# Part of the weights' low parts moved to VectorE, and earlier first quads, in the feed-forward products of two transformer blocks

## What is computed

```python
def conv_ffn(h, w_up, conv_w, conv_b, w_down):
    u = causal_dwconv(h @ w_up, conv_w, conv_b)
    g, val = jnp.split(u, 2, axis=-1)
    return (jax.nn.silu(g) * val) @ w_down
...
def swiglu(h, w_gate, w_up, w_down):
    return (jax.nn.silu(h @ w_gate) * (h @ w_up)) @ w_down
```

## Time and profile before

| what | value |
|---|---|
| median of 3 runs | 3294.6 us |
| lowest, highest | 3288.72, 3298.83 us |
| profiled execution: span | 3309.4 us |
| profiled execution: time of its own beside the span | the page gives none |
| mean granted TensorE clock | 0.930 |
| TensorE busy | 2912.6 us, 88% |
| GpSimd busy | 2220.5 us, 67%; 2220.1 of it in 884 low parts of 2522 ns on average |
| ScalarE busy | 1167.9 us, 35% |
| VectorE busy | 1128.3 us, 34% |
| moved by DMA | 598.17 MB, mean 181 GB/s |

### The profile page before, as it was taken

How to read it: one execution, slowest core, us unless ns; L and a number is a source line. 1 busy time by engine, 2 the same in 40 slices (tenths; PEclk the granted TensorE clock), 3 DMA queues, 4 the chain that set the end, 5 groups by cost and what they waited for, 6 DMA issues and landing times.

```text
span 3309.4 us, 54043 instructions
## 1 busy us (share of the span) xinstructions
PE 2912.6 (88%) x21608; PEld 2795.5 (84%) x21608; DVE 1128.3 (34%) x1286; ACT 1167.9 (35%) x1286; POOL 2220.5 (67%) x889
## 2 busy tenths in 40 slices
PE   4657879896789999999997976698898999999997
PEld 4657769775779999999997975598798999999997
DVE  4688771256855444422213032302102000001222
ACT  2222223332233433334443443233333333333443
POOL 2455768353758889878884843085476888887885
PEclk8778999798999999999998987698999999999999
DMA  7976765432746666545552542053243554554452
GB/s 218 351 267 241 272 250 207 166 142 81 261 176 226 229 219 238 191 164 179 187 180 90 189 129 90 8 221 129 102 164 129 180 187 179 181 187 165 178 184 96
DMA packets 112195, 598.17 MB, mean 181 GB/s; under 512 B 23340, under 2 KB 25388, under 8 KB 54860
## 3 DMA queue, kind: packets, MB, share of 16 engines
q1 hardware_dynamic: 92736, 570.84, 47.4%
q10 hardware_dynamic: 19340, 25.59, 2.7%
HBM read 581.98 MB, written 14.40 MB: 180 GB/s over the span
## 4 chain that ended last, share of the span: by engine, by line
PE 66%; issue 17%; POOL 11%; DVE 5%; ACT 1%; DMA 1%; ACTq 0%; POOLq 0%; DVEq 0%; SPq 0%
PE ps L825 20%; PE ps L827 20%; PE ps L829 20%; POOL w_lo L358 11%; PE ps L884 2%; PE ps L977 1%; PE ps L950 1%; DVE work L1281 1%; PE ps L966 1%; PE ps L841 0%; PE ps L839 0%; PE ps L843 0%; PE ps L954 0%; DVE work L1383 0%; DVE work L1252 0%
## 5 line engine op out<-in xcount | busy, mean ns | idle before, releaser
L358 POOL TENSOR_TENSOR w_lo<-raw,w_hi 128x1024 fp32r<-128x1024 f32 x884 | 2220.1, 2522 | 1054.5 <-ACT w_hi L379 1052.7
L825 PE MATMUL ps<-a_hi,w_hi 128*128 128x256 f32 x6512 | 1882.4, 289 | 236.9 <-DVE a_lo L1273 113.2
L827 PE MATMUL ps<-a_lo,w_hi 128*128 128x256 f32 x6512 | 1871.8, 287 | 0.0
L829 PE MATMUL ps<-a_hi,w_lo 128*128 128x256 f32 x6512 | 1870.7, 287 | 0.5 <-issue 0.5
L825 PEld LDWEIGHTS ps<-a_hi,w_hi 128*128 128x128 f32 x6512 | 1281.2, 197 | 251.6 <-issue 235.7
L379 ACT CAST w_hi<-raw 128x1024 fp32r<-128x1024 f32 x884 | 916.6, 1047 | 1589.8 <-PE ps L829 1080.8
L827 PEld LDWEIGHTS ps<-a_lo,w_hi 128*128 128x128 f32 x6512 | 1281.5, 197 | 0.2
L829 PEld LDWEIGHTS ps<-a_hi,w_lo 128*128 128x128 f32 x6512 | 1280.0, 197 | 0.7 <-issue 0.7
L1216 DVE SCALAR_TENSOR_TENSOR arena<-arena,small 128x1024 f32<-128x1024 f32 x150 | 388.9, 2628 | 105.4 <-DMA arena<-ada 104.5
L1332 DVE TENSOR_TENSOR a_lo<-arena,a_hi 128x1024 fp32r<-128x1024 f32 x44 | 112.7, 2565 | 364.4 <-ACT a_hi L662 364.4
L1652 DVE TENSOR_TENSOR arena<-ps,work 128x512 f32 (+1 forms) x22 | 15.2, 692 | 488.4 <-ACT work L792 488.4
(11 more groups left out here) (126 smaller groups left out, 1183.9 us busy)
## 6 DMA issues: line engine op xcount, KB each, us to landing
raw<-stream SPq DMA_DIRECT2D x442, 1024.0 KB, 4.8
arena<-ada SPq DMA_DIRECT2D x192, 512.0 KB, 4.6
arena<-memT SPq DMA_DIRECT2D x4, 512.0 KB, 7.9
res<-xT SPq DMA_DIRECT2D x1, 2048.0 KB, 20.8
rel_rows<-arena ACTq DMA_DIRECT2D x1, 2048.0 KB
mem_high<-a_hi ACTq DMA_DIRECT2D x1, 2048.0 KB, 46.6
mem_low<-a_lo ACTq DMA_DIRECT2D x1, 2048.0 KB, 24.6
k_spill<-arena ACTq DMA_DIRECT2D x4, 512.0 KB, 5.7
```

What stands on the lines that cost most here:

```text
L358: pool.tensor_tensor(w_lo[:, slot], raw[:, tile_slot, part * HALF:(part + 1) * HALF], w_hi[:, slot].bitcast(F32), ALU.subtract).then_inc(l ...
L825: pe.matmul(o, w_hi[:, slot, w], a_hi[:, c0 + k, :], start=first and k == 0 and f % 2 == 0, stop=False, skip_group_check=True)
L827: pe.matmul(o, w_hi[:, slot, w], a_lo[:, c0 + k, :], start=False, stop=False, skip_group_check=True)
L829: mm = pe.matmul(o, w_lo[:, slot, w], a_hi[:, c0 + k, :], start=False, stop=last and k == 1, skip_group_check=True)
```

## The change

Half of the low parts in the streams up, down, gu and down2 are made by VectorE: those with h % 8 of 2, 3, 6 and 7 (all four stages begin at a multiple of 8). The semaphore lo_ready becomes two, lo_dve and lo_pool, with tables of how many of each engine's low parts there are up to half h. TensorE waits for the low part alone, which implies the high part. SyncE's loops are cut so that the counts fit, without a change in the order of its transfers. VectorE's low parts stand at fixed places in its program: two before the norm, and then, in the up stage, two between group g-1's gate and group g's convolution, and two between that convolution and the next gate; in the down stages two after each a_lo. In ScalarE's down() the first two quads wait for their own groups and for TensorE to be done with the a_hi chunks that they overwrite, instead of for the last group.

```diff
+LOW_ON_DVE = {"up": (0, 0, 1, 1, 0, 0, 1, 1), "down": (0, 0, 1, 1, 0, 0, 1, 1),
+              "gu": (0, 0, 1, 1, 0, 0, 1, 1), "down2": (0, 0, 1, 1, 0, 0, 1, 1)}
+ON_DVE = [bool(LOW_ON_DVE.get(_name, (0,) * 8)[_i % 8]) for _name, _n in STREAM for _i in range(2 * _n)]
+DVE_COUNT = [sum(ON_DVE[:_h + 1]) for _h in range(len(ON_DVE))]
+POOL_COUNT = [_h + 1 - DVE_COUNT[_h] for _h in range(len(ON_DVE))]
...
-                    sp.wait_ge(lo_ready, t * 2 - 2 * RAW + 2)
+                    h, ahead = 2 * t - 2 * RAW + 1, 2 * step
+                    for low, count in ((lo_dve, DVE_COUNT), (lo_pool, POOL_COUNT)):
+                        if count[h] != (count[h - 2] if h > 1 else 0):
+                            more = 0 if i is None else count[h + ahead] - count[h]
+                            sp.wait_ge(low, i * more + count[h] if more else count[h])
...
             def down(name):
                 base = H0[name]
-                if name == "down":
-                    act.wait_ge(hid_ready, 22)
-                else:
-                    for G in (G0["gu"] + 20, G0["gu"] + 21):
-                        act.wait_ge(evac[G % 2], G // 2 + 1)
-
-                act.wait_ge(half_used, base)
-                hidden_high(0)
-                hidden_high(1)
+
+                def hidden_there(n):
+
+                    if name == "down":
+                        act.wait_ge(hid_ready, 2 * n)
+                    else:
+                        for G in (G0["gu"] + 2 * n - 2, G0["gu"] + 2 * n - 1):
+                            act.wait_ge(evac[G % 2], G // 2 + 1)
+
+                for n in range(2):
+                    hidden_there(n + 1)
+                    act.wait_ge(half_used, base - 6 + 2 * n)
+                    hidden_high(n)
                 his(base + 4, 4)
 
                 for n in range(2, 22):
+                    if n <= 10:
+                        hidden_there(n + 1)
                     act.wait_ge(half_used, base + 4 * (n - 1))
                     hidden_high(n)
                     his(base + 4 * n, 4)
...
-            def wait_half(n):
-
-                pe.wait_ge(hi_ready, n)
-                pe.wait_ge(lo_ready, n)
-
+            def wait_half(h, i=None, step=0):
+
+                low, count = (lo_dve, DVE_COUNT) if ON_DVE[h] else (lo_pool, POOL_COUNT)
+                n = count[h] if i is None else i * (count[h + step] - count[h]) + count[h]
+                pe.wait_ge(low, n)
...
+            def lows(a, b, i=None, step=16):
+
+                for h in range(a, b):
+                    if ON_DVE[h]:
+                        dve.wait_ge(hi_ready, h + 1 if i is None else i * step + (h + 1))
+                        dve.tensor_tensor(w_lo[:, h % SLOTS], raw_half(h), w_hi[:, h % SLOTS].bitcast(F32),
+                                          ALU.subtract).then_inc(lo_dve, 1)
...
+                    if n:
+                        lows(H0[name] + 4 * n, H0[name] + 4 * n + 4)
...
+            lows(H0["up"], H0["up"] + 4)
             norm("ffn", lambda c: res[:, c, :], lambda c: mod[:, 3, c:c + 1], lambda c: mod[:, 4, c:c + 1])
...
+            hu = H0["up"]
+            lows(hu + 4, hu + 12)
             up_conv(0)
+            lows(hu + 12, hu + 20)
             up_conv(1)
+            lows(hu + 20, hu + 24)
             up_gate(0)
             PER_TURN = 16
 
-            def up_turn(i):
-                for p in range(2):
-                    up_conv(2 + p, i, i * PER_TURN)
-                    up_gate(1 + p, i)
+            def up_turn(g0, i=None):
+                for g in range(g0, g0 + 2):
+                    lows(hu + 8 * g + 8, hu + 8 * g + 12 if g < 21 else hu + 8 * g + 10, i)
+                    up_conv(g, i, None if i is None else i * PER_TURN)
+                    if g < 21:
+                        lows(hu + 8 * g + 12, hu + 8 * g + 16, i)
+                    up_gate(g - 1, i)
 
             before = steps[0]
             with dve.Fori(0, 8) as i:
                 last_slice_rows(i)
-                up_turn(i)
+                up_turn(2, i)
             assert steps[0] - before == PER_TURN
-            steps[0] = before
-            with dve.Fori(8, 10) as i:
-                up_turn(i)
-            steps[0] = before + 10 * PER_TURN
+            steps[0] = before + 8 * PER_TURN
+            up_turn(18)
+            up_turn(20)
             up_gate(21)
+            lows(H0["down"] + 2, H0["down"] + 4)
             ada_mod(5)
             down("down", 0, gate=5)
...
+            lows(hg + 4, hg + 12)
             swiglu(0)
+            lows(hg + 12, hg + 16)
             with dve.Fori(0, 10) as i:
-                for p in range(2):
-                    swiglu(1 + p, i)
+                for g in range(1, 3):
+                    lows(hg + 8 * g + 8, hg + 8 * g + 12, i)
+                    swiglu(g, i)
+                    lows(hg + 8 * g + 12, hg + 8 * g + 16, i)
+            lows(hg + 176, hg + 178)
             swiglu(21)
+            lows(hg + 178, hg + 180)
             down("down2", 22)
```

More of the change, by code:

```diff
@@ L337, in _, with stream_tiles @@
                         sp.dma_start(ada_slot(s // 2 % 2), ada[n]).then_inc(ada_landed[s // 2 % 2], 16)
[L338 to L343, removed]
+            def stream_tiles(a, b):
+                turns = (b - a) // 4
+                with sp.Fori(0, turns) as g:
+                    for s in range(4):
+                        stream_tile(a + s, i=g)
+                for t in range(a + 4 * turns, b):
+                    stream_tile(t)
+            stream_tiles(165, T0["down"] + 6)
+            stream_tiles(T0["down"] + 6, T0["win2"])
+            for t in range(T0["win2"], T0["win2"] + 6):
+                stream_tile(t)
+            stream_tiles(T0["win2"] + 6, T0["gu"])
+            for t in range(T0["gu"], T0["gu"] + 6):
+                stream_tile(t)
+            stream_tiles(T0["gu"] + 6, TILES)
             for q in range(4):
@@ L353, in _, with low_part, low_parts @@
             pool.memset(ones[:, :], 1.0).then_inc(ones_ready, 1)
[L355 to L366, removed]
+            def low_part(h, i=None, step=0):
+                pool.wait_ge(hi_ready, h + 1 if i is None else i * step + (h + 1))
+                pool.tensor_tensor(w_lo[:, h % SLOTS], raw_half(h), w_hi[:, h % SLOTS].bitcast(F32),
+                                   ALU.subtract).then_inc(lo_pool, 1)
+            def low_parts(name, a, b):
+                h0, period = H0[name], 16
+                n = (b - a) // period
+                if n >= 2:
+                    with pool.Fori(0, n) as i:
+                        for h in range(h0 + a, h0 + a + period):
+                            if not ON_DVE[h]:
+                                low_part(h, i, period)
+                    a += n * period
+                for h in range(h0 + a, h0 + b):
+                    if not ON_DVE[h]:
+                        low_part(h)
+            for name, n in STREAM:
+                low_parts(name, 0, 2 * n)
         @block.scalar
@@ L1095, in step @@
                             pe.wait_ge(mod_ready, len(ADA_ORDER))
[L1096 to L1097 removed]
+                        wait_half(base_n + s, i, 8)
+                        half_T(base_n + s, outs[half][cg], par * 4 + 2 * kp, first and kp == 0,
                                last and kp == 1)
```

86 lines of the change are left out of this document (45 added, 41 removed).

## The result

The changed kernel takes 3381.69 us (median of 4 runs, 3379.91 to 3388.58), the kernel before in the same series 3292.02: a ratio of 1.0271, 95% interval 1.0253 to 1.0289, so about 90 us slower. The forecast was 3393, range 3340 to 3420.

A forecast was written before the change was run, and what follows sets the result against it. TensorE was taken to bound the kernel, with no low part late in the long stretches. Plain groups 18, groups behind ada rows 78 and down starts 1, taken as 98 us, on 3294.6 gave 3393 us, range 3340 to 3420.

The forecast's parts named there:

- TensorE bounds the down and gate/up stages: Down and gate/up: TensorE is busy throughout, so moving low parts off GpSimd has cost and gain 0.
- The early waits gain nothing: Down starts: ScalarE's queue has the last SiLU and two high parts ahead of the first quads; gain of the wait 0.
- Rival D: Down starts: early quads end standing of 7.48 and 5.13 us, giving 3279; chance 0.05 together with Rival E.
- The convolution starts 2.1 us late: Up stage, plain groups: low(8g+11) delays the convolution; stalls 0.7 and 0.6, 1.4 us per group, 13 groups, 18 us.
- Exclusion between VectorE and GpSimd: Up stage: a two-input VectorE instruction and a GpSimd one reading SBUF exclude each other throughout; without it about 60, not 98.
- Rival A: Up stage: no exclusion between VectorE and GpSimd, so only low(8G+12) is late behind the rows; 3355 us, chance 0.13.
- The rows go late: Up stage, eight turns: late ada rows delay SyncE's transfers and low parts; stalls 4.0 and 3.3, with clock 78 us.
- The clock: Up stage behind ada rows: long stalls lower TensorE's clock, between one and two 1.6 us losses per pair, taken 2.5.
- The signs: Up-stage trace: waits 70 us or more, paired 3 to 5 us stalls, plain groups about 24.4 us; other stages keep times.
- Rival B: Up stage: ada rows stay in time, leaving only 15 to 29 us; 3310 to 3324, chance 0.08.
- Rival C: Up stage: late weight tiles feed back, with clock losses at every stall, +115 to +150; 3410 to 3445, chance 0.12.
- Rival E: Whole kernel: no change, needing low(8g+11) through within 1.5 us of its half's release; chance 0.05 together with Rival D.

The follow-up runs named there:

- run 1: The changed kernel with all low parts back on GpSimd, leaving the early waits and recut semaphores: 3292.39 us, ratio 0.9977 to the kernel before.
- run 2: The changed kernel with only the up stage's low parts back on GpSimd: 3290.48 us, ratio 0.9991 to the kernel before.
- run 8: As run 7, but half of the low parts of down, gate/up and second down on VectorE: 3271.42 us, ratio 0.9937 to the kernel before.
- run 10: The edits of run 6 and run 7 together, half of all four stages' low parts on VectorE: 3274.72 us, ratio 0.9940 to the kernel before.
- run 7: All low parts on GpSimd, first quads of each down product moved ahead on ScalarE and VectorE: 3274.36 us, ratio 0.9944 to the kernel before.
- run 4: The changed kernel without the up stage's 32 ada rows and their transfers (incomplete computation, timing only): 3311.83 us, ratio 1.0051 to the kernel before.
- run 3: The changed kernel with low(8g+11) moved behind group g's convolution on VectorE: 3334.7 us, ratio 1.0121 to the kernel before.
- run 9: As run 4, with low parts of up halves 8g+14 and 8g+15 back on GpSimd: 3301.42 us, ratio 1.0028 to the kernel before.
- run 5: The changed kernel with each turn's third and fourth ada row moved behind group G's convolution: 3363.09 us, ratio 1.0207 to the kernel before.
- run 6: The changed kernel's work with VectorE's up stage reordered, low(8g+11) behind the convolution and ada rows spread out: 3290.23 us, ratio 0.9992 to the kernel before.

## Why the prediction was right, point by point

*TensorE bounds the down and gate/up stages, so GpSimd's relief is worth nothing there.* Shown by runs 1, 2, 8 and 10, and by the stretches after.

*The early waits gain nothing, ScalarE's order holds the quads.* Shown by runs 1 and 7. Rival D named its own condition, a first quad cast before the last SiLU, and this change doesn't meet it; run 7 does. Its price, 12.6 us and a clock loss behind each start, 16 in all, was 18 as measured.

*The convolution starts 2.1 us late and eats the slack.* 2.22 against 0.24. The stall was put at 1.4 per plain group, and a plain group takes 1.09 more in run 4 (24.13 against 23.04) and 0.9 at the end of the up stage: with some 0.5 and 0.4 in place of 0.7 and 0.6, and 0.1 behind each. The chain was counted right to 0.2 us, but against a slack of 1.5 us an error of 0.2 is a third of what is left over. The runs allot it as predicted: run 3 removes it, run 9 removes its second half.

*Exclusion between VectorE and GpSimd.* After, the pair of operations on GpSimd takes 5.74 us and that on VectorE 4.96, and run 9 prices it. Taken singly, GpSimd's first low part ends at 1129.59, and VectorE's, begun at 1129.05, ends 1.08 us after that (1130.67); GpSimd's second ends at 1132.93, VectorE's second again 1.08 us after it. The Trainium skill, on its page "SBUF — State Buffer", section "Who interferes with whom", has the ports that the two engines share as an exclusive lock, which a VectorE instruction with two SBUF inputs contends for with a GpSimd one that reads SBUF. The trace agrees, with the 1.08 us twice. Rival A, no exclusion, is out.

*The rows go late and take SyncE's queue and the low parts with them.* Shown by runs 4 and 5 for the two stalls apart. The third transfer leaves at 20.3 where 20.9 was forecast, the fourth at 23.7 (24.4), the fourth row is used at 30.4 (31.2), and TensorE starts half 8G+10 at 32.9 (34.0). The stalls were put at 4.0 and 3.3 and measured 3.6 and 2.9 on average over the eight turns (53.8 us together, with 0.4 that follows in five of them). The averages hide a spread that the forecast doesn't have: the first stall is 5.4 and 5.0 us in the first two turns and 2.8 to 3.6 in the others, the second 2.1 to 4.7. No run shows what makes it, so that the averages came so near is in part luck.

*The clock.* It was put at 2.5 us a turn, chosen between one and two losses of 1.6. Matmuls at the lower clock, which start 0.21 us apart instead of 0.12, add up to 19.9 us more in the eight turns, 2.5 a turn (2.1 to 3.0 in single turns).

*The sum.* 18 + 78 + 1 was forecast for the stalls with their clock. Measured: plain groups 13.1 (10.6 of gaps, the rest the 0.1 behind each), long stalls 53.8 and 2.2 for the same 0.1, clock 19.9, less 1.0 at the up stage's start and end, which were shorter than before: together the up stage's 88.0. The term that was most too large is the plain groups', 5 of the 9 us. The long stalls' was 2 too large, the clock's was right, and the 1 us at the down starts did not come (7.24 and 5.15 us against 7.48 and 5.13).

*The signs.* The plain groups' 24.13 us, the pairs of stalls, the fourth row after its group's end and the unchanged other stages came as named. One sign was missed: TensorE's waits in the up stage were to come to 70 us or more, and the profile's waits on low parts are 56.8 (29.5 + 27.3). Rivals B, C and E did not come about.

## What to carry to other kernels

Before you move work to an idle engine, see what stands behind it in that engine's queue and how much slack the chain through it has: here 1.2 us of work in front of a convolution with 1.5 us of slack, in a stage where the engine relieved was never waited for. A queue that issues transfers passes a consumer's delay on to all transfers behind it. An early wait is worth something only if the engine's program reaches it early; moving the instruction was worth 18 us, moving its wait none.

## What the runs showed of the hardware

What the clock does behind a stall of 2.8 to 5.4 us differs from turn to turn. After 2.87 us of standing up to 1320.2 the granted clock is 0.50 for the next 3.8 us; after nearly the same standing (2.79 us) up to 1263.2 it is 1.00 for as long:

```profile
1320.20:1324.00 3.80, 3.80 (x18) 3.80 (x19) 3.65 (x8) 0.00 (x0) 0.00 (x0) 0.50 1.00 405
```

```profile
1263.20:1267.00 3.80, 3.80 (x32) 3.80 (x33) 3.65 (x8) 0.00 (x0) 0.00 (x0) 1.00 1.05 427
...
1273.70:1277.00 3.30, 3.28 (x15) 3.29 (x16) 3.30 (x2) 0.38 (x1) 3.28 (x1) 0.50 0.00 0
```

There it fell at the next, longer stall (4.71 us) instead. In run 4, with gaps of 0.4 and 0.5 us alone, it stayed at 1.00 from 1050 to 1365. And the exclusion can be free: in run 6 VectorE's gates take 1452 ns on average and its low parts 1700, against 679 and 1860 in the changed kernel's up stage, with TensorE busy throughout.
